# Sevenfold products for layer 1's output and for three couples of query and key tiles of the last projection

## The reference

```python
for l in range(2):                       # first_block
    px = split_cols(norm_and_shift(x) @ w_in[l])      # 20 tiles of 128 columns
    attn = windowed_attention(...)
    y = concatenate([attn * silu(g_att), conv * silu(g_conv), fourier * silu(g_four)]) @ w_out[l]
    x = x + gate * y
x = rms_norm(x, final_g)
n = rmsnorm(x, g_mix)                    # second_block
aq, ak, av, iq, ik, iw, bq, bk, bv, mq = split(n @ w_in)      # 49 tiles
bq, bk = rope(bq), rope(bk)
y_a = dsa_attention(rope(aq), rope(ak), av, ...)      # top-k of 64 keys for each token
y_b = dilated_attention(bq, bk, bv); y_m = memory_attention(mq, mem)
h = x + merged(sigmoid(n @ w_gate), y_a, y_b, y_m) @ w_out
out = rmsnorm(h + hier_moe(h), g_final)
```

## Time and profile before

| | |
|---|---|
| median of 3 executions | 1033.65 us (1033.62 to 1034.15) |
| the profiled execution | 1033.84 us, span 1032.0 us |
| PE, DVE, ACT, GpSimd busy | 1007.3, 473.5, 348.2, 65.3 us |
| granted TensorE clock, mean | 0.998 of full speed |
| DMA | 227.51 MB, mean 220 GB/s |

### The profile page before, as it was taken

The page is one execution under the profiler, slowest core; times in us unless marked ns, Lnnn a source line. Parts: engine busy times, 40 slices in busy tenths (PEclk is TensorE's granted clock), DMA queues, the critical chain, the costliest instruction groups (busy, mean ns, idle before and its releaser), DMA issues.

```text
span 1032.0 us, 14552 instructions
## 1 busy us (share of the span) xinstructions
PE 1007.3 (98%) x5388; PEld 708.8 (69%) x5388; DVE 473.5 (46%) x1310; ACT 348.2 (34%) x843; POOL 65.3 (6%) x124
## 2 busy tenths in 40 slices
PE   6999999999999999999999999999999999999996
PEld 2468554547887777888888877799998844444442
DVE  5559836456356665355844524953522510000004
ACT  5224134335053247245553124742121411111112
POOL 0060000032200000000000000000000020000000
PEclk9999999999999999999999999999999999999999
DMA  9972125762234332444344342048657799999996
GB/s 362 420 304 86 42 81 198 290 247 82 83 137 149 123 108 77 153 176 157 136 157 164 123 183 103 2 167 328 244 200 306 270 388 422 419 420 421 421 420 250
DMA packets 33938, 227.51 MB, mean 220 GB/s; under 512 B 4577, under 2 KB 4849, under 8 KB 8112
## 3 DMA queue, kind: packets, MB, share of 16 engines
q1 hardware_dynamic: 30784, 214.97, 53.1%
q10 hardware_dynamic: 1920, 9.80, 2.6%
q0 software_dynamic: 1168, 1.85, 0.5%
HBM read 222.15 MB, written 8.41 MB: 223 GB/s over the span
## 4 chain that ended last, share of the span: by engine, by line
PE 90%; DVE 5%; DMA 3%; issue 1%; ACT 1%; DVEq 0%; SPq 0%; POOL 0%; POOLq 0%; ACTq 0%
PE lin L614 16%; PE lin L1267 9%; PE sc L733 6%; PE sc L630 6%; PE aux L614 5%; PE aux L1267 5%; PE aux L1154 4%; PE sc L838 4%; PE lin L802 3%; PE aux L868 3%; PE sc L1232 3%; PE lin L854 3%; PE sc L614 3%; PE lin L630 3%; PE sc L1021 3%; DVE UN L2106 2%
## 5 line engine op out<-in xcount | busy, mean ns | idle before, releaser
L614 PE MATMUL lin<-H,ring 128*128 128x256 f32 (+1 forms) x752 | 166.7, 384 | 0.0
L614 PEld LDWEIGHTS lin<-H,ring 128*128 128x128 f32 x752 | 142.7, 190 | 23.1 <-issue 4.2
L733 PE MATMUL sc<-H,ring 128*128 128x512 f32 (+1 forms) x192 | 67.3, 496 | 0.0
L2106 DVE SCALAR_TENSOR_TENSOR UN<-UN,cols 128x512 f32<-128x512 f32 (+1 forms) x120 | 66.7, 629 | 0.0
L1480 ACT ACTIVATE SP<-lin 128x512 f32<-128x512 f32 (+2 forms) x88 | 42.1, 486 | 72.1 <-PE lin L854 71.9
L2018 DVE CUSTOM_DVE_ANT_0 SP<-sc,CW,SK 128x512 f32<-128x512 f32 (+1 forms) x48 | 31.8, 662 | 55.4 <-PE sc L838 55.4
L1491 ACT ACTIVATE SP<-SP,ST 128x513 f32<-128x513 f32 (+4 forms) x88 | 53.9, 612 | 6.5 <-DVE ST L2021 6.2
L733 PEld LDWEIGHTS sc<-H,ring 128*128 128x128 f32 x192 | 34.8, 189 | 30.3 <-issue 25.6
L2581 DVE TENSOR_TENSOR PR<-lin,PR 128x512 f32<-128x512 f32 x8 | 5.5, 692 | 93.5 <-PE lin L1267 93.5
L838 PE MATMUL sc<-PR 64*128 64x256 f32 (+3 forms) x240 | 42.2, 434 | 2.9 <-DVE ST L2018 2.1
L1154 PE MATMUL aux<-Y,ring 128*128 128x256 f32 x192 | 41.8, 379 | 0.0
(11 more groups left out here) (460 smaller groups left out, 1710.8 us busy)
## 6 DMA issues: line engine op xcount, KB each, us to landing
ring<-w_stream SPq DMA_DIRECT2D x119, 1024.0 KB, 6.0
SP<-w_stream SPq DMA_DIRECT2D x14, 1024.0 KB, 20.5
UN<-w_stream SPq DMA_DIRECT2D x10, 1024.0 KB, 18.6
PR<-w_stream SPq DMA_DIRECT2D x8, 1024.0 KB, 17.4
CW<-w_stream SPq DMA_DIRECT2D x8, 1024.0 KB, 16.5
X<-w_stream SPq DMA_DIRECT2D x8, 1024.0 KB, 19.1
Y<-w_stream SPq DMA_DIRECT2D x8, 1024.0 KB, 18.7
PR<-ada_in SPq DMA_DIRECT2D x5, 1024.0 KB, 26.4
```

The source lines that it names most:

```text
L614: m = mm(dst, w[:, k, :], rhs(k), start=n == 0, stop=n == KT - 1)
L733: m = mm(bank[:, 0:ns * SEQ], filling["w"][:, k, :], H[:, 0:ns, k, :], start=k == 0, stop=k == KT - 1)
L2106: ins = v.scalar_tensor_tensor(out=CV[:, t, 0:ns, :], in0=u, scalar=w, in1=CV[:, t, 0:ns, :], op0=ALU.mult, op1=ALU.add)
```

## The change

Layer 1's output runs through `paired_out` too, as four pairs with halves of 128 tokens; GpSimd sums its weights after layer 1's sinks, the first two pairs at once, the others after DVE's four token sums. The joins to X, and the order in which its tiles are finished and squared, are those of layer 0. In the last projection three couples of two units (four tiles) run as 14 quarter products on halves of 128 tokens, even and odd ones, into the banks `sc` and `aux`. ACT copies five partial products of each unit, DVE joins three and sums the weights, four sums a unit, two of them written over the unit in the ring or kept in `Y` and `MORE`. The half turns of the four tiles come after all copies of the couple, and DVE's sums for the next couple's second unit stand between its second and third rope. The token sums are moved from tile 20 to tile 5. The pieces below are of PE's program, then ACT's, GpSimd's and DVE's.

```diff
-                if layer == 0:
-                    paired_out(0)
-                    paired_out(2)
-                else:
-                    projected_out((L, "out"), lambda k: YB[:, k, 0:ns, :], n, lambda n: pe.wait_ge(gated, KT * layer + n + 1),
-                                  MIX_ORDER)
+                paired_out(4 * layer)
+                paired_out(4 * layer + 2)
...
+            def paired_queries(c):
...
+                for x in range(2):
+                    w[x] = unit_of_pair()
...
+                    if c:
+                        pe.wait_ge(quarter_added, b_added(c - 1, x, 3))
+                    quarter(b_banks(c, x)[0], w[x][:, 0, lo], HB[:, 0, 0:4, :]).then_inc(quarter_made, 1)
+                for x in range(2):
+                    quarter(b_banks(c, x)[1], w[x][:, 0, hi], HB[:, 0, 4:8, :]).then_inc(quarter_made, 1)
+                for x in range(2):
+                    pe.wait_ge(quarter_read, b_read(c, x, 1))
+                    pe.wait_ge(tokens_mixed, V_TOKENS + 4)
+                    pe.wait_ge(weights_mixed, B_WEIGHTS + 8 * c + 4 * x + 3)
+                    quarter(b_banks(c, x)[0], B_T[c % 2][x][1], s2, start=False).then_inc(quarter_made, 1)
...
+                    quarter(b_banks(c, x)[2], B_T[c % 2][x][0], s1).then_inc(quarter_made, 1)
...
+                    quarter(b_banks(c, x)[0], w[x][:, 1, lo], s3, start=False).then_inc(quarter_made, 1)
...
+                    quarter(b_banks(c, x)[2], w[x][:, 1, hi], s4, start=False).then_inc(quarter_made, 1)
...
+                    quarter(b_banks(c, x)[0], B_T[c % 2][x][2], HB[:, 1, 4:8, :], start=False).then_inc(quarter_made, 1)
...
+                elif t in COUPLES:
+                    c = COUPLES.index(t)
+                    for x in range(2):
+                        act.wait_ge(quarter_made, b_at(c, x, 1))
+                        fn(b_tiles(c, x)[0][0], b_banks(c, x)[0], ACT.Copy).then_inc(quarter_read, 1)
...
+                    for x in range(2):
+                        act.wait_ge(quarter_added, b_added(c, x, 3))
+                        half_turned(PR[:, AT[t + 2 * x + 1], :]).then_inc(half_in, 1)
+                    for x in range(2):
+                        act.wait_ge(quarter_read, b_read(c, x, 4))
+                        half_turned(PR[:, AT[t + 2 * x], :]).then_inc(half_in, 1)
...
-                if name == "l0":
-                    for n in range(4):
-                        if n == 2:
-                            pool.wait_ge(tokens_mixed, 8)
-                        mixed(len(PAIRED) + n, FIRST_OUT + n, *LO_HI[::-1], S_OUT[n])
+                for n in range(4):
+                    if n == 2:
+                        pool.wait_ge(tokens_mixed, 4 * layer + 8)
+                    mixed(len(PAIRED) + 4 * layer + n, FIRST_OUT[layer] + n, *LO_HI[::-1], S_OUT[4 * layer + n])
...
+                if t == COUPLES[0] - 2:
+                    mixed_queries(0, 0)
+                    mixed_queries(0, 1)
+                if t in COUPLES:
...
+                        v.tensor_tensor(to, to, b_banks(c, x)[1], ALU.add).then_inc(quarter_added, 1)
+                    if c + 1 < len(COUPLES):
+                        mixed_queries(c + 1, 0)
...
+                    for n, tile in enumerate((t + 1, t + 3, t, t + 2)):
+                        rope(None, PR[:, AT[tile], :], t2("cos"), t2("sin"), True, turned=len(ROPED1) + 4 * c + n + 1)
+                        if n == 1 and c + 1 < len(COUPLES):
+                            mixed_queries(c + 1, 1)
...
-                if t == BK:
+                if t == IQ:
```

More of the change, by code:

```diff
@@ L434, in out_banks, with out_half @@
         def out_banks(p):
[L436 removed]
+            n = P if p >= 4 else SEQ
+            return lin[p % 2][:, 0:n], sc[:, p % 2, 0:n], sc[:, p % 2, 512:512 + n]
+        def out_half(x, p, s):
+            return x[:, :, 0, s * P:(s + 1) * P] if p >= 4 else x[:, :, s, :]
         def out_at(p, product):
@@ L629, in quarter @@
                 for i in range(4):
-                    m = mm(dst, left[:, i * P:(i + 1) * P], right[:, i, :], start=start and i == 0, stop=i == 3, skip_group_check=True)
+                    part = left[:, i * P:(i + 1) * P] if len(left.shape) == 2 else left[:, i // 2, i % 2 * P:i % 2 * P + P]
+                    m = mm(dst, part, right[:, i, :], start=start and i == 0, stop=i == 3, skip_group_check=True)
                     if i < 3:
@@ L763, in memory_keys @@
                     m.then_inc(keys_ready, 1)
[L765 to L768, removed]
             def ada_step(bank, k0):
@@ L1057, in _ @@
                         paired_values((t - BV) // 4)
+                    continue
+                if t in COUPLES:
+                    paired_queries(COUPLES.index(t))
+                if any(a <= t < a + 4 for a in COUPLES):
                     continue
@@ L1667, in _ @@
             for k in range(KT):
-                act.wait_ge(aux_taken, turn["l1", "out", k] + 1)
+                act.wait_ge(quarter_read, OUT_READ + out_final(KT + FINAL[k]))
                 if k >= 2:
@@ L1973, in _, with rope @@
             ropes = [0]
-            def rope(key, x, cos, sin, halves=False):
+            def rope(key, x, cos, sin, halves=False, turned=None):
                 b = ropes[0] % 2
                 ropes[0] += 1
-                if key is None:
+                if turned is not None:
+                    dve.wait_ge(half_in, turned)
+                elif key is None:
                     dve.wait_ge(half_in, ropes[0])
@@ new lines, in _ @@
+                base, tokens = 4 * layer, 4 * layer + 4
+                first_tokens, second_tokens = (out_half(YB, base, a) for a in range(2))
+                t1_, t3_, t2_, t4_ = T_OUT[layer]
+                dve.wait_ge(gated, KT * layer + KT)
+                dve.wait_ge(tokens_mixed, tokens + 1)
+                v.tensor_tensor(t2_, second_tokens[:, 0:4, :], t1_, ALU.subtract).then_inc(tokens_mixed, 1)
+                v.tensor_tensor(t3_, second_tokens[:, 0:4, :], second_tokens[:, 4:8, :], ALU.subtract).then_inc(tokens_mixed, 1)
@@ new lines, in _, with joined @@
+                dve.wait_ge(tokens_mixed, tokens + 2)
+                v.tensor_tensor(t4_, first_tokens[:, 0:4, :], t2_, ALU.subtract).then_inc(tokens_mixed, 1)
+                def joined(p, product, bank, s, t, before=None):
+                    dve.wait_ge(quarter_made, OUT_PART + out_at(p, product))
+                    if before:
+                        dve.wait_ge(quarter_read, OUT_READ + out_at(p, before))
+                    x = X[:, 0, t, s * P:(s + 1) * P] if p >= 4 else X[:, s, t, :]
+                    v.scalar_tensor_tensor(out=x, in0=out_banks(p)[bank], scalar=MOD[:, p // 4, 2 * KT + t, 0:1] if p >= 4 else MOD[:, 0, 2 * KT + t, s:s + 1],
+                                           in1=x, op0=ALU.mult, op1=ALU.add).then_inc(quarter_read, 1)
@@ new lines, in _ @@
+                for c in (0, 2):
+                    for p in (c, c + 1):
+                        joined(base + p, 1, 0, 0, 2 * p)
+                    for p in (c, c + 1):
+                        joined(base + p, 5, 2, 1, 2 * p + 1)
+                    for p in (c, c + 1):
+                        joined(base + p, 2, 1, 0, 2 * p, before=1)
+                    if c:
+                        add_squares([0, 1], 2)
+                    for p in (c, c + 1):
+                        joined(base + p, 6, 0, 1, 2 * p)
+                    if c:
+                        add_squares([2, 3], 2)
+                    for p in (c, c + 1):
+                        joined(base + p, 7, 0, 1, 2 * p + 1, before=5)
+                    for p in (c, c + 1):
+                        joined(base + p, 3, 2, 1, 2 * p, before=6)
+                    if c:
+                        add_squares([4], 2)
+                    joined(base + c, 4, 0, 0, 2 * c + 1)
+                    if c:
+                        add_squares([5], 2)
+                    joined(base + c + 1, 4, 0, 0, 2 * c + 3)
```

199 lines of the change are left out of this document (127 added, 72 removed).

## The result

The changed kernel takes **1038.71 us** (median of five, 1037.71 to 1040.13) against 1033.78 us (1033.62 to 1034.15) for the kernel before on the same chip: a ratio of 1.0049, 95% interval 1.0035 to 1.0064. It is slower by 4.9 us, where 1034.9 us was forecast, 1.1 us slower, in a range that ended at 1038.2. The profiled execution took 1038.44 us with a span of 1036.6 us, against 1033.84 and 1032.0 before: 4.6 us more from span to span.

The account below looks back on a forecast made before the run. PE alone was taken to bound both rewritten stages before the change. Terms -2.7 + 0.8 - 4.0 + 7.2 = +1.3 us on the profiled 1033.84 us, median 0.19 lower, gave 1034.9 us; range 1030.2 to 1038.2 us.

Parts of the forecast that it names:

- term 4: Last projection: PE waits of 0.9, 3.5, 2.1 and 0.7 us on ACT's queue and DVE's sums, together +7.2 us.
- Term 1: Layer 1's output: 28 quarter products take 25.03 us against 27.82, with no wait inside, -2.7 us.
- Term 2: Layer 1's attention: GpSimd's sums slow DVE's softmax scalings, so ACT's last exponentials and PE's transposes come later, +0.8 us.
- Term 3: Last projection: three couples at 12.52 us of PE work instead of 13.84, stepped operands at no cost, -4.0 us.
- (b): Rival: bursts cost more, each couple's wait feeds the next and GpSimd's sums delay all three softmax pairs; 1037.3 us, chance 0.29.
- (a): Rival: queues absorb the bursts in the last projection, no PE gap over 0.5 us; 1027.8 us, chance 0.15.
- (c): Rival: products 1, 2 and 4 run slower reading every second float of H; at worst +15 us, 1050 us, chance 0.04.

Follow-up runs that it names:

- output-only kernel: Layer 1's output in quarters as in the change, the last projection as in the kernel before: 1031.31 us against 1033.78.
- Without the sums: The output-only kernel, with each of GpSimd's sixteen sums for layer 1 cut to 4 columns: 1032.25 us.
- reads first: The change, with ACT's reads of product one of couples 1 and 2 moved ahead of the half turns of the two whole tiles before: 1029.88 us.
- weights later: The change, with DVE's sums for the next couple's second unit behind the fourth rope: 1033.55 us; the same kernel again for the second trace: 1033.90 us.
- three edits: The change, with ACT's reads of product one first, product five ahead of six, and ACT's tile 32 copy between half turns behind couple 2: 1028.39 us.
- filled waits: The change, with 12 and 8 matmuls that nothing reads put on PE in the waits before product six of couples 1 and 2: 1035.71 us.

## Why the prediction was wrong

It named the waits, their places and their releasers, and it mis-sized one term above all, term 4: **what a wait costs.** Term by term, against the sum of +1.3 us:

- **Term 1, layer 1's output (-2.7): right, -2.3.** The quarters ran at 0.893 us as read from the late gates, with no wait inside. But the group of split first products took 0.1 us extra in the first couple of pairs and 0.3 in the second (1.89 and 2.11 us for two quarters where others take 1.79), and I had allowed 0.1 for the turn: 25.5 us by the chain, not 25.1.
- **Term 2, GpSimd's sums beside the attention (+0.8): the rows right, the price wrong, 0.0.** The scalings took 2.16, 2.22 and 1.90 us for 0.88, inside the 1.5 to 2 us foretold or just above. The Trainium skill (GPSIMD Engine Reference, Key points) has the contention, and this trace agrees once more. The failing step is "so ACT's last exponentials end 0.8 later": they ended 0.3 us later (the table load behind them starts at 400.37 in the output-only kernel, at 400.06 before), and by ACT's next reading of scores 0.05 us of it was left (402.17 against 402.12). Without the sums the output starts at the same time.
- **Term 3, PE's work (-4.0): right within 0.3, -3.7.** A couple without waits takes 12.59 us (reads first) against 13.84; 0.09 us of each is the stepped operand, which I had put at nothing.
- **Term 4, the waits (+7.2): the idle time right, 6.7; the term wrong, +10.9.** Foretold 0.9, 3.5, 2.1, 0.7; measured 0.78, 3.15, 2.01, 0.73, with the releasers named, and couple 0's wait from DVE's weight sums. That DVE's unit between the ropes has a share in it was right too: 1.1 us of each of the two. The step that failed is that I put a wait down as its idle time and nothing more. A wait of PE costs about 0.26 us more than its idle time even where the clock holds: the second trace of weights later has 14.95 - 12.59 - 2.09 = 0.27 us over, three edits 13.09 - 12.59 - 0.23 = 0.27. Of this 0.16 is that the last matmul before it is seen to its end (0.275 us a row, where rows follow one another every 0.11), and 0.10 lies in the row behind it (3.84 us at 524.60 in three edits, 3.74 for the same 32 rows at 529.93 in the change); what the 0.10 is made of is not shown. Couple 0's wait costs 0.23, the other three 0.26 each: 1.0 us. And behind the two long ones PE's clock fell, for 1.64 and 1.63 us (17.64 - 12.59 - 3.15 - 0.26, and 16.49 - 12.59 - 2.01 - 0.26): 3.3 us. The filled waits gave back just that, 1.63 and 1.64 us, and the two traces of weights later differ by 1.61.

The sum by these numbers is -2.3 + 0 - 3.7 + 10.9 = +4.9 us; the two stages show 7.3 - 2.3 = +5.0, so 0.1 us stays unassigned. 4.6 us reached the end of the span. Term 4 alone was 3.7 us too low. Term 2, 0.8 us too high, hid part of that: without this luck the forecast would have been 0.8 us further off.

Of the rivals, (b) came nearest in time (1037.3) and is wrong in kind: the waits did not feed one another, and three of the four were a little shorter than forecast (the last was 0.73 us for 0.7). (a) is refuted as said, by four gaps where it allowed none over 0.5 us, and (c) is true at 0.015 us a quarter, under 2% of its worst case. On that point the Trainium skill (SBUF — State Buffer, the note on cachelines in the section Door 1) says that two hits in a 16-byte line are enough for full bandwidth, and every second float makes two hits; the runs say almost (1.82 us for two quarters against 1.79).

Could the clock have been read from the trace of before? In part. Between its first and its last matmul PE never stands idle there for more than 1.4 us, and the granted clock is 1.00 behind that. But PE is also idle for the first 8.7 us, until its first weights are there (view of PE's waits, kernel before: us in total, times, longest; then two rows of PE's timeline, and two windows of 2 us each):

```profile
PE lin L884 <- DMA ring<-w_stream: 8.7, 1, 8.7
...
PE lin L938 <- ACT H L1540: 1.4, 1, 1.4
```

```profile
8.74 9.63 PE L884 MATMUL lin<-ring,UN 128*128 128x512 f32 x16 [8.74 <-DMA ring<-w_stream]
...
19.09 1.88 PE L884 MATMUL lin<-ring,UN 128*128 128x512 f32 x4
```

```profile
10.00:12.00 2.00, 2.00 (x3) 0.77 (x3) 1.61 (x4) 1.44 (x4) 0.00 (x0) 1.00 0.94 248
...
16.00:18.00 2.00, 2.00 (x6) 0.95 (x5) 1.78 (x3) 1.45 (x3) 0.00 (x0) 1.00 1.07 451
```

In the first window 3 rows run, whole or in part, in the second 6 of the same form, with PE busy throughout. The 16 rows take 9.47 us from the first start to the next instruction's (8.74 to 18.21), where the later pace of 0.43 us a row (four in 1.71 us, from 19.09 to the next instruction's start at 20.80) gives 6.84: 2.6 us more behind a long idle time. The view gives the granted clock as 1.00 in both windows, so that this is the clock is my reading of the halved pace and not shown. Still, it is a bound from above that the prediction could have used: it put waits of 3.5 and 2.1 us where no row showed what the clock does after more than 1.4, and up to 2.6 us for each of the two would have put the upper end at 1043 us and held the result. The Trainium skill (TensorE: Matmul & The Clock Gate, the section HAM oscillation) describes this danger: waits between bursts of matmuls bring the half clock back, and it is paid again at each of them. The traces here agree, at 1.6 us a drop, but already behind 2.01 us, where the Trainium skill's example has waits of 3 to 5 us, and not behind every wait: after one of 2.09 us the clock held.

## What to carry to other kernels

A scheme that trades matmuls for passes over the result moves its work in bursts to the engine that reads the accumulators; place the one read that the next product waits for ahead of the bulk work in that engine's queue, and check the place in the queue, not the engine's load (ACT was busy for 34% of the changed kernel's span and still held PE up). Price a stall of PE above its idle time, with the clock behind it as soon as it is longer than any that the profile shows harmless. And where one engine waits for another's queue, work saved ahead of the wait is worth nothing until the queue itself gets shorter or is put in another order.

## What the hardware did that I had not expected

- PE's granted clock fell behind idle times of 3.15, 2.41, 2.08 and 2.01 us, and stayed at 1.00 behind 0.94, 0.91, 0.81 and 0.78 us. It did not fall behind 2.09 us in one execution of a kernel in which it fell behind 2.08 us in another. So one kernel has times in two groups some 1.5 us apart: 1033.4 to 1033.8 and 1034.7 to 1035.6 us in one experiment, 1031.8 to 1031.9 and 1033.1 to 1033.7 in another; what decides between them is not shown. A single time of such a kernel says little. The kernel before has one such time too (1035.33 us at a mean granted clock of 0.997, among fifteen of which the others are 1033.5 to 1034.2), and no trace shows its reason.
- The drop does not always begin with the first matmul: in couple 2 of the change the windows show 0.85 for the first 2 us behind the wait and 0.57 for the 3.3 us that follow, when PE was busy again.
- A wait of PE costs about 0.26 us above its idle time even where the clock holds, so that many short waits are dearer than their sum.
- A moving operand that reads every second float costs 0.015 us on a quarter of 0.893 us.
- Matmuls that nobody reads, 24 rows in one wait and 16 in the other, made the kernel 3.0 us faster.
